# Splitting streamed weights into two fp32r halves: from GpSimd's own loop to fixed places in ScalarE's and VectorE's programs

## The reference

```python
# first block
h = rms_norm(x, norm_mix); aq, ak, av, bq, bk, bv, cq = split(h @ w_in)
out_a = diff_attention(...); out_b = dilated windows, 3 groups; out_c = memory_attention(...)
x = x + sum(sigmoid(h @ w_gate + b_gate) * (branches @ w_branch)) @ w_out
x = x + (silu(h2 @ w_ffn_gate) * (h2 @ w_ffn_up)) @ w_ffn_down
# second block, two layers
x = x + 0.5 * swiglu(rmsnorm(x), ffn1_w1, ffn1_w3, ffn1_w2)
x = x + concat(hgrn2_mixer(...), multiscale_pool(...)) @ w_out
x = x + mem_cross_attention(rmsnorm(x), rmsnorm(mem), wq, wkv, wo)
x = x + 0.5 * swiglu(rmsnorm(x), ffn2_w1, ffn2_w3, ffn2_w2)
```

## Time and profile before

| | |
|---|---|
| median of 3 runs | 3566.22 us (3566.14 to 3566.43) |
| profiled execution: span from first to last instruction | 3564.0 us |
| TensorE busy | 3361.2 us, 94% |
| VectorE busy | 1794.4 us, 50% |
| ScalarE busy | 550.6 us, 15% |
| GpSimd busy | 1998.9 us, 56% |
| mean granted TensorE clock | 0.975 |
| HBM read | 309.58 MB, 87 GB/s |

### The profile page before, as it was taken

How to read it: one execution, slowest core, us unless ns; L and a number is a source line. 1 busy time by engine, 2 the same in 40 slices (tenths; PEclk the granted TensorE clock), 3 DMA queues, 4 the chain that set the end, 5 groups by cost and what they waited for, 6 DMA issues and landing times. The chain is left out here.

```text
span 3564.0 us, 40617 instructions
## 1 busy us (share of the span) xinstructions
PE 3361.2 (94%) x15102; PEld 2706.5 (76%) x15102; DVE 1794.4 (50%) x1948; ACT 550.6 (15%) x933; POOL 1998.9 (56%) x1112
## 2 busy tenths in 40 slices
PE   8889999999999999999789999999999978999998
PEld 6657776767888888887676888888888867778886
DVE  6665665446452455228854555235422776455521
ACT  2432332221000100010112100010001021220000
POOL 5324434646666666663463666666666435456664
PEclk9989999999999999999899999999999989999999
DMA  4212222222322222221221222222222212222222
GB/s 133 92 62 85 87 83 77 98 92 89 99 95 95 95 94 97 93 97 59 77 83 60 89 94 98 96 92 98 94 95 98 71 59 84 76 71 94 97 98 71
DMA packets 88818, 313.36 MB, mean 88 GB/s; under 512 B 9984, under 2 KB 10496, under 8 KB 88448
## 3 DMA queue, kind: packets, MB, share of 16 engines
q1 hardware_dynamic: 82080, 294.69, 24.7%
q10 hardware_dynamic: 6624, 17.03, 1.6%
HBM read 309.58 MB, written 2.10 MB: 87 GB/s over the span
## 5 line engine op out<-in xcount | busy, mean ns | idle before, releaser
L788 POOL TENSOR_TENSOR wlo<-raw,whi 128x1024 fp32r<-128x1024 f32 x554 | 1334.8, 2409 | 1523.1 <-PE ps L817 1520.9
L815 PE MATMUL ps<-x_hi,whi 128*128 128x512 f32 x2816 | 1125.5, 400 | 13.8 <-DVE x_lo L1265 7.9
L817 PE MATMUL ps<-x_hi,wlo 128*128 128x512 f32 x2816 | 1103.4, 392 | 0.0
L816 PE MATMUL ps<-x_lo,whi 128*128 128x512 f32 x2816 | 1103.1, 392 | 0.0
L779 POOL TENSOR_SCALAR whi<-raw 128x1024 fp32r<-128x1024 f32 x554 | 682.3, 1232 | 9.2 <-DMA raw<-in_weights 9.2
L815 PEld LDWEIGHTS ps<-x_hi,whi 128*128 128x128 f32 x2816 | 533.5, 189 | 140.1 <-DVE x_lo L1265 14.5
L816 PEld LDWEIGHTS ps<-x_lo,whi 128*128 128x128 f32 x2816 | 533.9, 190 | 113.2 <-issue 5.8
L817 PEld LDWEIGHTS ps<-x_hi,wlo 128*128 128x128 f32 x2816 | 532.8, 189 | 113.2
L817 PE MATMUL ps<-h_hi,wlo 128*128 128x512 f32 x880 | 346.7, 394 | 0.0
L815 PE MATMUL ps<-h_hi,whi 128*128 128x512 f32 x880 | 346.7, 394 | 0.0
L816 PE MATMUL ps<-h_lo,whi 128*128 128x512 f32 x880 | 346.7, 394 | 0.0
(11 more groups left out here) (249 smaller groups left out, 3444.1 us busy)
## 6 DMA issues: line engine op xcount, KB each, us to landing
raw<-in_weights SPq DMA_DIRECT2D x554, 512.0 KB, 3.2
bias<-in_biasB ACTq DMA_DIRECT2D x16, 384.0 KB, 3.2
bias<-in_biasA ACTq DMA_DIRECT2D x16, 256.0 KB, 3.3
x_res<-in_x SPq DMA_DIRECT2D x8, 256.0 KB, 7.3
x_res<-in_x ACTq DMA_DIRECT2D x1, 2048.0 KB, 9.2
out_x<-x_res SPq DMA_DIRECT2D x8, 256.0 KB, 2.1
mem_raw<-in_mem ACTq DMA_DIRECT2D x1, 1024.0 KB, 4.8
mem_raw2a<-in_mem ACTq DMA_DIRECT2D x2, 512.0 KB, 4.2
```

Of the source, the lines that this page charges most:

```text
L788: pool.tensor_tensor(wlo[c % RING][:, :], raw[c % RAW][:, :], whi[c % RING][:, :].bitcast(F32), ALU.subtract).then_inc(sems["unit_ready"], 1)
L815: pe.matmul(out, hi, xhi, start=start, stop=False)
L816: pe.matmul(out, hi, xlo, start=False, stop=False)
L817: return pe.matmul(out, lo, xhi, start=False, stop=stop)
```

## The change

GpSimd's block is deleted. ScalarE makes `whi` with a Copy activation and VectorE makes `wlo` with the same tensor_tensor as before, which now writes over the raw buffer: `wlo[k]` lies at the address of `raw[k]`. There are four raw buffers instead of three, and with `wlo` gone as a buffer of its own the whole takes 12 KB less of each partition. A load now waits for `unit_free` of unit `u-4`, that is, for TensorE, and no longer for the split of `u-3`.

Where ScalarE and VectorE do a unit's halves is fixed by a new step `unit`: `open_units` puts it into the list ahead of the job, two units ahead of the last one that the job reads (`AHEAD = 2`). In the feed-forward loop the halves of two units stand at the head of each chunk, for ScalarE before its `silu`, for VectorE before it takes out `ffn_g`.

```diff
-RAW = 3
+AHEAD = 2
...
     def job(self, tile0, nk, /, **a):
+        self.open_units((tile0 + nk - 1) // UT + AHEAD)
         j = self.njobs
...
+    def open_units(self, upto):
+        while self.next_unit <= upto:
+            self.step("unit", u=self.next_unit)
+            self.next_unit += 1
...
+        s.open_units(t0 // UT + AHEAD - 1)
         step("ffn", n=n, unit0=t0 // UT)
+        s.next_unit += 2 * NF
...
+        raw_at = top[0]
+        raw = [fixed(f"raw{k}", [P, UT * P]) for k in range(RING)]
+        wlo = [nc.alloc_sbuf_tensor_at(f"wlo{k}", [P, UT * P], F32R, offset=raw_at + 4 * KB * k) for k in range(RING)]
         whi = [fixed(f"whi{k}", [P, UT * P], F32R) for k in range(RING)]
-        wlo = [fixed(f"wlo{k}", [P, UT * P], F32R) for k in range(RING)]
...
             def load(i, c):
-                if not (isinstance(i, int) and i * step + c < RAW):
-                    sp.wait_ge(sems["unit_ready"], i * step + (c - RAW + 1))
+                if not isinstance(i, int):
+                    sp.wait_ge(sems["unit_free"], i * RING + (c - RING + 1))
...
-        @block.gpsimd
...
+            def high(u, i=0):
+                act.wait_ge(raw_landed[u % RING], i * 16 + 16 * (u // RING + 1))
+                copy(whi[u % RING][:, :], raw[u % RING][:, :]).then_inc(sems["unit_hi"], 1)
...
                     def silu(i):
                         for jj in range(2):
+                            high(a["unit0"] + AHEAD + 2 * jj, i)
+                            high(a["unit0"] + AHEAD + 2 * jj + 1, i)
                             act.wait_ge(sems["fg"], i * 2 + (fg0 + jj + 1))
...
+            def low(u, i=0):
+                dve.wait_ge(sems["unit_hi"], i * RING + (u + 1))
+                dve.tensor_tensor(wlo[u % RING][:, :], raw[u % RING][:, :], whi[u % RING][:, :].bitcast(F32),
+                                  ALU.subtract).then_inc(sems["unit_ready"], 1)
...
+                        low(u0 + AHEAD + 2 * jj, i)
+                        low(u0 + AHEAD + 2 * jj + 1, i)
```

More of the change, by code:

```diff
@@ L78, in __init__ @@
         self.njobs = 0
+        self.next_unit = 0
         self.nsq = 0
@@ L540 @@
     "act": ["sq", "xh", "sd", "msq", "mh", "msd", "hsq", "hsd", "exp", "pt", "v", "ohi", "gate", "yhi", "silu",
-            "sigm", "lam_exp", "lb_exp", "hgs"],
+            "sigm", "lam_exp", "lb_exp", "hgs", "unit_hi"],
     "dve": ["setup", "xs", "xl", "rstd", "ms", "ml", "rstdm", "evac", "x", "hrec", "hn", "max", "nmax", "pn", "pvd",
             "olo", "y", "ylo", "fg", "fu", "fm", "fhh", "fhl", "fin", "hprep", "qkt", "lvd", "ho", "hgated",
-            "pooled", "ptmp"],
-    "pool": ["unit_hi", "unit_ready"],
+            "pooled", "ptmp", "unit_ready"],
 }
@@ L556, in program @@
         d_x = [ctx.enter_context(nc.semaphore(f"d_x{m}")) for m in range(DC)]
-        raw_landed = [ctx.enter_context(nc.semaphore(f"raw_landed{k}")) for k in range(RAW)]
+        raw_landed = [ctx.enter_context(nc.semaphore(f"raw_landed{k}")) for k in range(RING)]
         engine_of = {n: e for e, ns in RAISES.items() for n in ns}
@@ L583, in fixed @@
             return t
-        raw = [fixed(f"raw{k}", [P, UT * P]) for k in range(RAW)]
+        raw_at = top[0]
+        raw = [fixed(f"raw{k}", [P, UT * P]) for k in range(RING)]
+        wlo = [nc.alloc_sbuf_tensor_at(f"wlo{k}", [P, UT * P], F32R, offset=raw_at + 4 * KB * k) for k in range(RING)]
         whi = [fixed(f"whi{k}", [P, UT * P], F32R) for k in range(RING)]
-        wlo = [fixed(f"wlo{k}", [P, UT * P], F32R) for k in range(RING)]
         X = fixed("x_res", [P, DC, T])
@@ L740, in _ @@
         def _(sp):
-            step = RAW * RING
             def load(i, c):
-                if not (isinstance(i, int) and i * step + c < RAW):
-                    sp.wait_ge(sems["unit_ready"], i * step + (c - RAW + 1))
-                src = dram["weights"][bass.ds(i * step + c, 1)].rearrange("a p n -> (a p) n")
-                sp.dma_start(raw[c % RAW][:, :], src).then_inc(raw_landed[c % RAW], 16)
+                if not isinstance(i, int):
+                    sp.wait_ge(sems["unit_free"], i * RING + (c - RING + 1))
+                src = dram["weights"][bass.ds(i * RING + c, 1)].rearrange("a p n -> (a p) n")
+                sp.dma_start(raw[c][:, :], src).then_inc(raw_landed[c], 16)
             for m in range(DC):
@@ L753, in _ @@
                     load(0, 0)
-            for c in range(1, step):
+            for c in range(1, RING):
                 load(0, c)
-            with sp.Fori(1, NU // step) as i:
-                for c in range(step):
+            with sp.Fori(1, NU // RING) as i:
+                for c in range(RING):
                     load(i, c)
-            assert NU % step
-            for c in range(NU % step):
-                load(NU // step, c)
+            for u in range(NU // RING * RING, NU):
+                sp.wait_ge(sems["unit_free"], u - RING + 1)
+                sp.dma_start(raw[u % RING][:, :], dram["weights"][u]).then_inc(raw_landed[u % RING], 16)
             for m in range(DC):
@@ L1058, in _ @@
                     act.activation(small[:, 12:20], small[:, 12:20], ACT.Exp).then_inc(*sig("lb_exp"))
+                elif kind == "unit":
+                    if a["u"] < NU:
+                        high(a["u"])
                 elif kind == "consts":
@@ L1243, in _ @@
                         .then_inc(*sig("setup", "lam"))
+                elif kind == "unit":
+                    if a["u"] < NU:
+                        low(a["u"])
                 elif kind == "masks":
```

## The result

The changed kernel takes **3509.4 us** (median of 4 runs, 3507.5 to 3509.8), the kernel before 3566.2 us beside it (3566.0 to 3566.4): ratio 0.984, 95% interval 0.9825 to 0.9853, 57 us or 1.6% faster. The forecast was 3524 us, 42 us of gain, with a range of 3498 to 3568. Its profiled execution spans 3507.8 us at a mean granted clock of 0.98, against 3564.0 us and 0.975.

What follows compares the result with a forecast made beforehand. TensorE bounds the nets; elsewhere VectorE's chains, held up by GpSimd on the shared port, make it wait. Terms -32 - 6 - 3 - 3 - 2.5 + 1 + 3 = -42.5 on 3564.0, plus 2.2, gave 3524 us, range 3498 to 3568.

Steps and rivals of the forecast that it cites:

- The scans: Both scans: contention relief and fewer cold restarts, less a third of the low halves, -16 us each, -32 together.
- restarts: Scans: where a gap closes, matmuls no longer restart at the low clock; 1.5 us each, three or four gaps, -5 a scan.
- the contention that goes: Scans: h_f 5.5, h_kt 5.0, h_suf 4.4, pooling sums 5.8 us freed from GpSimd, 20.7 a scan, all on the path.
- A attention: A attention: operations on the probabilities and the handover to the branch product gain, less low halves there; -6 us.
- B attention: B attention: some 45 low halves, one in twenty late by its whole 1.23 us; +3 us.
- the wait at 590: A 5.0 us wait at 590 us behind memory splits that meet GpSimd twice; -3 us.
- refreshes: Before each feed-forward net, the last residual chunk's refresh no longer meets GpSimd; about -0.5 us each, -2.5.
- entries: Entry of five feed-forward nets: one low half behind the norm's reciprocal stalls TensorE 0 to 0.5 us each; +1.
- Low halves in the chain: Slower rival: VectorE lags in the scans, so each low half delays what follows; up to +39 us, 3605 us; chance 0.11.
- More of the gaps close: Faster rival: few low halves count, relief reaches smaller groups; scans 27 each, A attention 12, rest 12; -78, 3488 us; chance 0.15.
- The waits stay: Rival: in A attention and scans, reciprocals, roots and a low half fill the gaps; 3559 to 3573 us; chance 0.10.
- Halves not ready: Rival: TensorE waits for units because ScalarE or VectorE is held up, 0.05 us each over 554 units; 3552 us; chance 0.10.

Runs made afterwards that it cites:

- both_left_out: Changed kernel with VectorE's low and ScalarE's high halves cut to 8 columns from the fifth unit on, shorter loads, TensorE's operand addresses kept: 3464.2 us.
- low_left_out: Changed kernel with only VectorE's low halves cut to 8 columns from the fifth unit on, shorter loads, TensorE's operand addresses kept: 3474.7 us.
- early_low_late: Changed kernel with the first three units' halves moved among the first norm's chunks and later low halves placed behind a job's evacuation: 3525.0 us.
- low_gpsimd: Changed kernel with the low halves back on GpSimd as two-operand tensor_tensor, high halves still on ScalarE: 3534.7 us.
- high_gpsimd: Changed kernel with the high halves back on GpSimd as one-operand tensor_scalar, low halves still on VectorE: 3518.5 us.

## Why the prediction was right, and where its steps were not

The cause was right: VectorE's two-operand instructions no longer meet GpSimd's, and only a part of the low halves lies on the path. The sizes were not. Over the whole kernel the relief is 102 us where the forecast's terms for it came to about 68, the low halves cost 35 (31.5 by spans) for some 25, and the high halves, put at nothing, cost 10 (14). The misses pull in different directions, and that they left the sum only 15 us off, just inside the forecast's own range of 3508 to 3542, is partly luck.

*The scans, -32 forecast, -46.9 measured.* The relief was summed to 51.4 (20.7 and 5 for restarts, twice); by before against both_left_out it is 31.9 + 36.6 = 68.5 us. The failed step is "the contention that goes": four groups in a window of 192 us made 20.7, and were to "stand for the smaller groups as well". Over the whole scan of 295 us it is 55.6: the same four groups lost 30 us, not 20.7, and the smaller ones 23, not nothing. "All of it on the path" failed the other way: 55.6 us of VectorE bought 19.6 us of TensorE's idle and 12.6 us at a better clock. The low halves were counted as 24 at a third, 9.8 us a scan; there are 40 at a quarter, 10.6 and 8.0. That size was right by two misses that cancelled. The high halves cost nothing in the first scan and 3.5 us in the second. Restarts: 5 a scan forecast; matmuls took 7.1 us less in the first and 9.2 in the second.

*A attention, -6 forecast, -6.2 measured.* Right as a sum, wrong in parts: relief 13.8 us, low halves 2.4, high halves 5.2, which stood at nothing with "at most 0.3 us for a tile". One stands ahead of a table load and a root whose reciprocal TensorE waits for, and costs 0.95 us there (6.83 for 5.88). That the parts gave the forecast's number was luck.

*B attention, +3 forecast, and the wait at 590, -3.* With the keys and values behind it the stage is 2.8 us longer: 5.8 of relief, 4.1 for the low and 4.5 for the high halves. The wait fell by 2.6 us, as forecast, but the rest grew.

*The start, memory and cross attention, -3; refreshes, -2.5; entries, +1.* The start gave 0.9: the last `x_lo` ended 9 us earlier, but three pairs of halves had been put behind all eight chunks. C attention with its output product and the two nets behind it gave 4.7, all the rest 0.3. The five entries cost 0.2 us each against low_left_out, 2.09 for the two low halves less 1.88 that the loop gave back; I had counted one low half.

*The rivals.* "Low halves in the chain" decides from 21 of 24 on the path; it was 10.6/1.22, about 9 of 40. Its milder case was summed wrong: three quarters of 29.5 less half of 20.7 is 12 us a scan, so 24 for both and not 12. "More of the gaps close" was right that the relief reaches the smaller groups, and wrong that few low halves count: its 78 us of gain, 27 a scan and 12 in A attention, were 57, 21.7 and 25.2, and 6.2. "The waits stay" was right about the longest wait: with no halves at all it is still 10.4 us. "Halves not ready": TensorE waited 14.4 us for `wlo`, 13.1 of them at the start; it came out elsewhere only when the halves were moved (early_low_late).

*What would show it.* `ffn_m`, the two halves and 663 matmuls came as said. The wait for `h_kt` was to fall below 8 and stayed at 11.6; the clock was to be above 0.9 and was 0.89 and 0.90. Those two signs failed although the gain was larger. TensorE's idle in the first scan fell from 43.8 to 29.2 us. The longest gap gave only 0.7 of these 14.6 us; the rest came mostly from the gaps of 2.5 to 7.5 us behind it (`vt_sb` 7.5 to 5.1, the one before the output product 5.7 to 2.8, two waits for `h_kt` of 3.5 and 2.5 gone). The other 7.1 us are matmuls at a better clock, 0.93 for 0.91 over the stage, where the forecast had 5.

Not settled: the sum of single prices. Two-operand work on GpSimd costs 56 us (low_gpsimd against low_left_out, by spans), one-operand work about 24 (high_gpsimd against after, 10, and the high halves' 14); the other 22 of 102 I put down to their working together, without a run that shows it; the ring and the loads are in it too.

## What to carry over

GpSimd is no free engine beside a busy VectorE: price its work by what VectorE's groups lose, over the whole stage and all groups (busy time against the same work undisturbed), and expect no more than a part of that back: in the first scan 32 of 55.6 us came back; over the whole kernel VectorE got some 530 us of its time back (1794.4 us busy before, 1359.7 in low_left_out, of which 95 are its narrow and first halves) and the kernel took some 90 us less. In the nets, where `ffn_m` alone lost 1.6 us each time, nothing waited for it. An engine that is idle on average still has moments when one more microsecond is on the path, ahead of a root or of the first job; a left-out run by stage finds them. Before such a run is believed, compare a stretch where nothing waits: if its matmuls have another pace, the edit changed more than it says.

## What the runs showed of the hardware

- A VectorE instruction with two operands in SBUF that starts inside a GpSimd instruction that reads SBUF ends after it: 1.53 for 0.69 us beside a tensor_scalar, 2.71 beside a tensor_tensor. In the kernel before, 185 such tensor_tensors of 512 columns started inside one of GpSimd's, and all of them ended 0.55 us behind it. One already under way is not slowed (0.69), nor is one that takes an operand from PSUM (0.69 inside GpSimd's tensor_tensor in low_gpsimd, 268 of them).
- Beside GpSimd's memsets two-operand instructions keep 693 and 1221 ns, and a one-operand 128x512 tensor_scalar goes from 427 to 874 ns.
- The pace of back-to-back 512-column matmuls at the full clock depended on the buffers that the weights were read from: 150/663, 150/651 and 150/657 us in three kernels with the same shapes and instruction counts. Whether the addresses do it or the reading of one buffer over and over, no run shows.
- ScalarE's 128x1024 copy takes 1055 ns, and each of the changed kernel's 82 table loads 1.28 us.
